# Decoder step: loading x in parallel buffers, taking the statistic of norm 0 before the modulation, and copying pass-through data later

## What is computed

```
mods = (silu(c) @ w_ada + b_ada).reshape(B, 16, 1024)        # 16 vectors per sequence
# layer 0
h = rmsnorm(x, norm_g[0,0]) * (1 + mods[1]) + mods[0]        # "norm 0"
a = h @ w_pw1 + b_pw1;  u = a[:, :1024] * sigmoid(a[:, 1024:])
y = silu(layernorm(depthwise_conv31(concat(state_conv, u)))) @ w_pw2
x = x + mods[2] * y
x = x + mods[5] * swiglu(rmsnorm(x) * (1 + mods[4]) + mods[3])
# then shared keys and values, layer 1: sparse attention and SwiGLU, a last norm
conv_sample = concat(state_conv, u)[:, -30:]                  # its first 22 rows are copies of state_conv
win_sample  = concat(state_win, new rows)                     # its first 256 rows are copies of state_win
```

## Time and profile before

| | us |
|---|---|
| median of 3 runs | 1905.48 (1901.27 to 1909.15) |
| profiled execution, own time | 1907.56 |
| its span | 1905.9 |
| TensorE busy | 1679.4 (88%) |
| VectorE busy | 914.8 (48%) |
| ScalarE busy | 561.5 (29%) |
| GpSimd busy | 270.9 (14%) |

### The profile page before, as it was taken

One profiled execution on the slowest core, in us unless ns is written; L12 is line 12 of the kernel. 1 busy time (PEld: TensorE's weight loads), 2 busy tenths in 40 slices (PEclk: granted clock), 3 DMA queues, 4 the chain that ended last, 5 costly groups with the idle time before them and its releaser, 6 DMA issues.

```text
span 1905.9 us, 30256 instructions
## 1 busy us (share of the span) xinstructions
PE 1679.4 (88%) x12409; PEld 1488.9 (78%) x12409; DVE 914.8 (48%) x1618; ACT 561.5 (29%) x1058; POOL 270.9 (14%) x384
## 2 busy tenths in 40 slices
PE   5788874497999999997988989988897999999995
PEld 2666653397999999997887965454497999999994
DVE  1479999755323232335224246756645323223333
ACT  2332221333222122222221355544423222122222
POOL 1002939120000000000210034432300000000000
PEclk8899987698999999998899999978998999999997
DMA  9399983051233222321322240020221233222311
GB/s 311 157 348 341 307 278 102 0 137 56 78 97 92 66 79 85 107 64 34 100 73 56 77 121 23 1 68 23 67 68 55 78 95 94 63 82 82 110 32 50
DMA packets 236591, 198.10 MB, mean 104 GB/s; under 512 B 6999, under 2 KB 196127, under 8 KB 236253
## 3 DMA queue, kind: packets, MB, share of 16 engines
q1 hardware_dynamic: 230448, 172.54, 29.4%
q0 software_dynamic: 5840, 23.30, 3.9%
q10 hardware_dynamic: 173, 0.39, 0.1%
HBM read 188.88 MB, written 11.20 MB: 105 GB/s over the span
## 4 chain that ended last, share of the span: by engine, by line
PE 71%; DVE 11%; issue 8%; ACT 4%; DMA 3%; DVEq 1%; POOL 1%; SPq 1%; ACTq 0%; POOLq 0%
PE ps L1444 58%; PE ps L1426 4%; PE ps L1752 2%; PE ps L1705 2%; DMA ada<-in_w_ada_dram 2%; DVE y L1117 2%; DVE wl L971 1%; PE ps L1631 1%; DVE r L1117 1%; PE ps L1472 1%; DVE r L995 1%; PE ps L1822 1%; DVE y L1122 1%; PE ps L1607 1%; DVE t L1005 1%
## 5 line engine op out<-in xcount | busy, mean ns | idle before, releaser
L1444 PE MATMUL ps<-Hh,wh 128*128 128x288 f32 x2128 | 470.8, 304 | 67.9 <-DVE Hl L1010 40.8
L1444 PE MATMUL ps<-Hl,wh 128*128 128x288 f32 x2128 | 465.4, 301 | 0.0
L1444 PE MATMUL ps<-Hh,wl 128*128 128x288 f32 x2128 | 464.2, 300 | 0.0
L646 ACT ACTIVATE wh<-raw 128x1024 fp32r<-128x1024 f32 (+1 forms) x173 | 192.9, 1116 | 828.2 <-PE ps L1444 805.8
L1444 PEld LDWEIGHTS ps<-Hh,wh 128*128 128x128 f32 x2128 | 351.5, 194 | 71.9 <-issue 70.5
L1444 PEld LDWEIGHTS ps<-Hl,wh 128*128 128x128 f32 x2128 | 351.9, 193 | 0.2
L1444 PEld LDWEIGHTS ps<-Hh,wl 128*128 128x128 f32 x2128 | 351.5, 193 | 0.2
L971 DVE TENSOR_TENSOR wl<-raw,wh 128x1024 fp32r<-128x1024 f32 (+1 forms) x173 | 225.1, 1301 | 255.5 <-ACT wh L646 255.0
L1444 PE MATMUL ps<-ah,wl 128*128 128x288 f32 x704 | 150.8, 296 | 0.0
L1444 PE MATMUL ps<-ah,wh 128*128 128x288 f32 x704 | 150.8, 296 | 0.0
L1444 PE MATMUL ps<-al,wh 128*128 128x288 f32 x704 | 150.7, 296 | 0.0
(11 more groups left out here) (273 smaller groups left out, 1958.5 us busy)
## 6 DMA issues: line engine op xcount, KB each, us to landing
ada<-in_w_ada_dram SPq DMA_DIRECT2D x64, 1024.0 KB, 7.6
raw<-in_ffn_w_up_dram SPq DMA_DIRECT2D x88, 512.0 KB, 3.8
raw<-in_ffn_w_down_dram SPq DMA_DIRECT2D x32, 704.0 KB, 4.6
raw<-in_conv_w_pw_dram SPq DMA_DIRECT2D x24, 512.0 KB, 8.5
raw<-in_w_kv_dram SPq DMA_DIRECT2D x12, 512.0 KB, 3.7
C<-in_cache_kv_dram POOLq DMA_DIRECT2D x32, 128.0 KB, 4.1
raw<-in_nsa_w_in_dram SPq DMA_DIRECT2D x8, 512.0 KB, 3.8
Cs<-in_cache_kv_dram SPq DMA_DIRECT2D x16, 256.0 KB, 3.9
```

The source lines that it names most:

```text
L646: A(wh[:, u % RING, 0:K, 0:w], raw[:, u % RING, 0:K, 0:w], ACT.Copy).then_inc(hi_ready, 1)
L1444: last = M(ps[0:w, 2 * s + h, 0:HT], wt[:, s, k, 0:w], rt[:, k, h * HT:(h + 1) * HT], start=(k == 0 and i == 0), stop=(k == K - 1 and i == 2))
```

## The change

The x blocks get a buffer each (two in `stage`, three in `xrows`, which lies in the still unused `Hl`), and all five are requested at the start. The two `state_conv` blocks reuse the first two buffers once blocks 0 and 1 are transposed. TensorE transposes the five x blocks in a row, does strip 0, block 5, the eight sums of squares in banks 4 and 5, strip 1 and its turn, block 6, then strips 2 and 3. ScalarE splits units 0 to 2 after the x blocks and squares x after strip 0. It takes the root before the results of strips 2 and 3. VectorE takes the reciprocal of norm 0 before it waits for the modulation. The two pass-through copies are requested behind GpSimd's wait for the first pw2 unit, ahead of the small tables, `w1k`, `w1v` and `C`.

```diff
@@ -94,7 +94,10 @@
...
 STRIPS_FIRST = 4
-STRIP_BLOCKS = [1, 2, 3, 4]
+ROW_BUF = [0, 1, 2, 3, 4, 0, 1]
+ROW_BANK = [0, 1, 2, 0, 1, 0, 1]
@@ -229,6 +232,7 @@
...
         xf = at("xf", [P, DC, T], rH)
+        xrows = at("xrows", [P, 3, D], rH + DC * T * 4)
         rF = region(2 * FHC * T * 4)
@@ -349,6 +353,7 @@
...
         stats = ps[:, 6:8, 0:HT]
+        stats0 = ps[:, 4:6, 0:HT]
@@ -381,6 +386,12 @@
...
         xi_rows = [P, P, P, P, TS, 120, 120]
+        def rows_in(bk):
+            n, k = xi_rows[bk], ROW_BUF[bk]
+            return stage[0:n, k, :] if k < 2 else xrows[0:n, k - 2, :]
         page_rows = a["cache_kv"].rearrange("n (q e) t h d -> n q e (t h d)", e=2)
@@ -493,31 +504,25 @@
...
             def load_rows(bk):
-                n = xi_rows[bk]
-                if bk >= 2:
-                    pool.wait_ge(S("xi_pe"), bk - 1)
+                if bk >= 5:
+                    pool.wait_ge(S("xi_pe"), bk - 4)
                 if bk < 4:
...
                     src = a["state_conv"].rearrange("l b t d -> (l b t) d")[120 * (bk - 5):120 * (bk - 4), :]
-                pool.dma_start(stage[0:n, bk % 2, :], src).then_inc(S(f"xi_in{bk % 2}"), 16)
-            load_rows(0)
-            load_rows(1)
+                pool.dma_start(rows_in(bk), src).then_inc(S(f"xi_in{ROW_BUF[bk]}"), 16)
+            for bk in range(5):
+                load_rows(bk)
             nc.gpsimd.memset(ones[:], 1.0).then_inc(S("const"), 1)
...
             nc.gpsimd.memset(u_p[:, :, 0:CW - 1], 0.0).then_inc(S("const"), 1)
-            for bk in range(2, 7):
+            for bk in range(5, 7):
                 load_rows(bk)
             pool.dma_start(pgt[:], a["page_table"].rearrange("b n -> (b n)").unsqueeze(0)).then_inc(S("pg_in"), 16)
-            pool.dma_start(o["conv_sample"][0, :, 0:CW - 1 - NT, :],
-                           a["state_conv"][0, :, NT:CW - 1, :]).then_inc(S("thru"), 16)
-            pool.dma_start(wss[:, 0:PAST, :], a["state_win"].rearrange("b s t h d -> b s (t h d)")).then_inc(S("thru"), 16)
@@ -546,6 +551,9 @@
...
             pool.wait_ge(ada_ev, 16 * DC)
+            pool.dma_start(o["conv_sample"][0, :, 0:CW - 1 - NT, :],
+                           a["state_conv"][0, :, NT:CW - 1, :]).then_inc(S("thru"), 16)
+            pool.dma_start(wss[:, 0:PAST, :], a["state_win"].rearrange("b s t h d -> b s (t h d)")).then_inc(S("thru"), 16)
             pool.dma_start(w2t[:], a["w_cmp2"].rearrange("t e d -> e t d")).then_inc(S("cb_in"), 16)
@@ -664,7 +672,7 @@
...
                 act.wait_ge(S("st_ck"), sums_done(st))
-                A(halves(r[:]), stats, ACT.Sqrt, scale=1.0 / D, bias=epst[:]).then_inc(S("st_rms"), 1)
+                A(halves(r[:]), stats if st else stats0, ACT.Sqrt, scale=1.0 / D, bias=epst[:]).then_inc(S("st_rms"), 1)
@@ -690,8 +698,6 @@
...
             A(rows0[0:72, 4, :], rows0[0:72, 4, :], ACT.Silu).then_inc(S("c_silu"), 1)
-            for u in range(SPLIT_AHEAD):
-                split_hi(u)
             act.wait_ge(S("vec_pe"), 2)
@@ -699,7 +705,7 @@
...
                 n = xi_rows[bk]
-                src = ps[:, 2 * (bk % 3) + 1, 0:4 * n].rearrange("p (c t) -> p c t", c=4)
+                src = ps[:, 2 * ROW_BANK[bk] + 1, 0:4 * n].rearrange("p (c t) -> p c t", c=4)
                 if bk < 5:
@@ -709,19 +715,21 @@
...
                 block_out(bk)
-                if bk in STRIP_BLOCKS:
-                    if bk == STRIP_BLOCKS[0]:
-                        act.wait_ge(S("vec_dve"), 3)
-                    s_ = STRIP_BLOCKS.index(bk)
-                    strip_out(s_, s_ - 1 if s_ else None)
-            strip_out(None, STRIPS_FIRST - 1)
+            for u in range(SPLIT_AHEAD):
+                split_hi(u)
+            act.wait_ge(S("vec_dve"), 3)
+            strip_out(0, None)
             act.wait_ge(S("xi_dve"), 5)
...
             block_out(5)
+            strip_out(1, 0)
             block_out(6)
             root(0)
+            strip_out(2, 1)
+            strip_out(3, 2)
+            strip_out(None, STRIPS_FIRST - 1)
             norm_hi(0)
@@ -973,6 +981,13 @@
...
                 g0, sh, sc = NORMS[k]
+                def inverse():
+                    dve.wait_ge(S("st_rms"), STAT_OF[k] + 1)
+                    V.reciprocal(r[:], r[:]).then_inc(S("st_r"), 1)
+                if k == 0:
+                    inverse()
                 dve.wait_ge(ada_ev, 2 * max(4 * (sh + 1), 4 * (sc + 1)))
@@ -990,10 +1005,9 @@
...
                                 ALU.mult).then_inc(S("n_s"), 1)
-                if k != 3:
-                    dve.wait_ge(S("st_rms"), STAT_OF[k] + 1)
-                    V.reciprocal(r[:], r[:]).then_inc(S("st_r"), 1)
-                    dve.wait_ge(S("st_r"), STAT_OF[k] + 1)
+                if k not in (0, 3):
+                    inverse()
+                dve.wait_ge(S("st_r"), STAT_OF[k] + 1)
                 dve.wait_ge(S("n_s"), 3 * k + 1)
@@ -1051,12 +1065,13 @@
...
             V.tensor_copy(badaT[:], ps[:, 7, 384:512]).then_inc(S("vec_dve"), 1)
-            for u in range(SPLIT_AHEAD):
-                split_lo(u)
             for bk in range(7):
+                if bk == 5:
+                    for u in range(SPLIT_AHEAD):
+                        split_lo(u)
                 dve.wait_ge(S("xi_pe"), bk + 1)
                 n = xi_rows[bk]
-                src = ps[:, 2 * (bk % 3), 0:4 * n].rearrange("p (c t) -> p c t", c=4)
+                src = ps[:, 2 * ROW_BANK[bk], 0:4 * n].rearrange("p (c t) -> p c t", c=4)
                 if bk < 5:
@@ -1467,9 +1482,9 @@
...
-            def sum_chunk(src, cc, done, n=DC):
+            def sum_chunk(src, cc, done, n=DC, bank=6):
                 for h in range(2):
-                    last = M(ps[:, 6 + h, 0:HT], ones[:], src[:, h * HT:(h + 1) * HT], start=(cc == 0), stop=(cc == n - 1))
+                    last = M(ps[:, bank + h, 0:HT], ones[:], src[:, h * HT:(h + 1) * HT], start=(cc == 0), stop=(cc == n - 1))
                 last.then_inc(done, 1)
@@ -1496,34 +1511,35 @@
...
                 n = xi_rows[bk]
-                pe.wait_ge(S(f"xi_in{bk % 2}"), 16 * (bk // 2 + 1))
-                if bk >= 3:
-                    pe.wait_ge(S("xi_dve"), bk - 2)
-                    pe.wait_ge(S("xi_act"), bk - 2)
+                pe.wait_ge(S(f"xi_in{ROW_BUF[bk]}"), 16 * (1 + bk // 5))
+                if ROW_BANK[bk] in ROW_BANK[:bk]:
+                    before = max(k for k in range(bk) if ROW_BANK[k] == ROW_BANK[bk])
+                    pe.wait_ge(S("xi_dve"), before + 1)
+                    pe.wait_ge(S("xi_act"), before + 1)
                 for cc in range(DC):
-                    last = tr(ps[:, 2 * (bk % 3) + cc // 4, (cc % 4) * n:(cc % 4 + 1) * n],
-                              stage[0:n, bk % 2, cc * P:(cc + 1) * P])
+                    last = tr(ps[:, 2 * ROW_BANK[bk] + cc // 4, (cc % 4) * n:(cc % 4 + 1) * n],
+                              rows_in(bk)[:, cc * P:(cc + 1) * P])
                 last.then_inc(S("xi_pe"), 1)
...
                 block_in(bk)
-                if bk in STRIP_BLOCKS:
-                    s_ = STRIP_BLOCKS.index(bk)
-                    if s_ == 0:
-                        pe.wait_ge(S("const"), 4)
-                        pe.wait_ge(S("vec_act"), 1)
-                        pe.wait_ge(S("vec_dve"), 3)
-                    strip(s_)
-                    if s_:
-                        turn_strip(s_ - 1)
+            pe.wait_ge(S("const"), 4)
+            pe.wait_ge(S("vec_act"), 1)
+            pe.wait_ge(S("vec_dve"), 3)
+            strip(0)
+            block_in(5)
+            pe.wait_ge(S("xi_dve"), 3)
+            pe.wait_ge(S("xi_act"), 3)
+            for cc in range(DC):
+                pe.wait_ge(S("st_sq"), cc + 1)
+                sum_chunk(sqb[:, cc, :], cc, S("st_ck"), bank=4)
+            strip(1)
+            turn_strip(0)
+            block_in(6)
+            for s_ in range(2, STRIPS_FIRST):
+                strip(s_)
+                turn_strip(s_ - 1)
             turn_strip(STRIPS_FIRST - 1)
-            pe.wait_ge(ada_ev, 4 * STRIPS_FIRST)
-            for cc in range(DC):
-                if cc == 2:
-                    block_in(5)
-                    block_in(6)
-                pe.wait_ge(S("st_sq"), cc + 1)
-                sum_chunk(sqb[:, cc, :], cc, S("st_ck"))
             pe.wait_ge(S("st_rms"), 1)
```

## The result

| | median us | runs |
|---|---|---|
| before | 1909.15 | 5 (1901.27 to 1910.40) |
| changed | 1921.61 | 5 (1918.34 to 1924.52) |

The ratio is 1.0076, 95% interval 1.0055 to 1.0097: slower by three quarters of a per cent. The profiled execution has a span of 1922.9 us, 17.0 more than before.

A forecast was written before the change was run, and what follows sets the result against it. The start was taken as bound in turn by transfers, a serial chain and VectorE's taps. 1907.6 - 11.0 + 16.1 + 1.8 = 1914.5 for the profiled execution; the median, 2.1 lower, was named 1913, range 1895 to 1921.

The forecast's parts named there:

- Part 1: First stage: computing the norm statistic ahead of the modulation takes 15.4 us off the path to the dense products.
- The delay of strip 3: First stage: strip 3's last half starts 4.4 us later than before, bounds 1.5 to 8.
- its first term: First stage: 0.6 MB more ahead of `ada` 1 at 387 GB/s makes strip 0 end 1.6 us later.
- Part 3: In pw2: the moved pass-through copies and q0's rest hold back unit 22's weights, so TensorE stands for 16.1 us.
- The gain at the dense products: End of the first stage: first dense product 11.0 us earlier (7.4 to 13.9), from 15.4 - 4.4.
- The memsets and the splits of units 0 to 2 cost nothing: First stage: memsets delayed some 2 us are not waited for before block 0; the splits' first user is the dense product.
- The stall at unit 22: In pw2: weights land near 432.5, are split at 434.8; TensorE, due at 418.7, stands 16.1 us (3 to 22.6).
- The restart: In pw2 after the wait for unit 22: TensorE restarts at the lower clock, costing 1.8 us (0 to 2).
- Rival 1: In pw2: copies stay hidden, unit 22 lands by 410 to 417, stall 0 to 1, time 1894 to 1896; chance 0.17.
- Rival 2: In pw2: stall ends with the large copy, landing 423, stall 6.6, restart 1, time 1902; chance 0.14.
- Rival 3: In pw2: q0's whole rest goes first, landing 437 to 440, stall 21 to 24, time 1917 to 1920; chance 0.18.
- Rival 4: First stage: strips 1 to 3 at lower clock, every load waited for; strip 3 11 late, gain 4, 1919; chance 0.09.

The follow-up runs named there:

- the experiment on what stands behind the copies: Changed kernel with `w1k`, `w1v` and `C` requested only when all pw2 units are done: 1913.46 us, ratio 1.0021 to the kernel before.
- the first experiment: Changed kernel with the two pass-through copies requested when strip 3 has been used, not at the first pw2 unit: 1901.15 us, ratio 0.9952 to the kernel before.

## Why the prediction was wrong

It named 1913 with a range to 1921, and the result was 1921.6, 0.6 beyond. (Its own sum, 1914.5 less 2.1, is 1912.4.) Its profiled execution was forecast at 1914.5 and took 1924.5. The stall and its place were right. The gain of the first stage was too high by 6.6 us, the stall too low by 1.9 and the restart by 1.1: 9.6 of the 10.0 us.

1. *What Part 1 removes*, 15.4 us: measured 15.3. Right.
2. *The delay of strip 3*, taken as 4.4 with bounds 1.5 to 8: measured 10.1. This is the step that failed, and it lay outside its own bounds. Of the missing 5.7 us 5.1 are its first term, the transfers ahead of `ada` 1, where "about half fits into the little-used first 10 us" left 1.6 us: strip 0's second half ran 6.7 us later (30.35 against 23.64). From there on the account fits. It had load 7 requested at 42.8 and landed at about 50; 5.1 us later is 47.9 and 55.1, and the chain has 47.36 and 54.82. The bytes were right: before strip 0's second half q0 moved 3.34 MB, against 2.10, so 1.24 MB more. The sharing was not: from 22 to 26 us `state_conv` took the larger half (0.61 MB of q0, 0.42 of q1), while both together went at 252 to 262 GB/s and not at 387. With `state_conv` later strip 0's second half came 4.7 us earlier than in the changed kernel (25.61). I had used this sharing in Part 3 and not here. The other 3.4 us, put at 2.8, lie behind strip 0, where the sums stand in front of strip 1; moving them brought the dense product forward by 4.1 us against the changed kernel. What bounds the stage was also put too simply: from 20 to 30 us TensorE was busy for 8.20 of the 10 us, and waited 1.80 us for one load.
3. *The gain at the dense products*, 11.0 us: 5.2, and 4.4 by unit 19's split, as the first three units ran 0.65 us longer.
4. *The memsets and the splits of units 0 to 2 cost nothing*: right. The small rows, which I had not counted as held back, came 4.6 us later (14.03, before 9.46). This too cost strip 0 nothing: with them early again its second half stayed at 30.36 (25.42 against 25.61 with `state_conv` late).
5. *The stall at unit 22*, 16.1 us: 18.0. The landing was forecast 33.3 us after the request and took 35.2. Both parts of it stood the test. The large copy ended 24.8 us after the request (forecast 22.3, bound 25.5), and its rest took 10.4 more (forecast 11). *The restart*, 1.8 (0 to 2): 2.9, above its bound.
6. *Rival 1*, the copies hidden in pw2, falls. The reading of the earlier trace rows was right and holds elsewhere: 450 packets of q0 beside 449 of q1. By the rule of the Trainium skill (DMA: Bandwidth & Descriptors, Queues, rings and completion order), a whole run of descriptors per turn, unit 22 would have landed within 18 us of its request, which is an estimate of the forecast. It took 35.2, and no trace here shows such runs between two queues that are both moving. *Rival 2* falls with the experiment on what stands behind the copies. *Rival 3* gave 1917 to 1920 by a stall of 21 to 24; the stall was 18. *Rival 4* had the right place and the right sign (a gain of 4, measured 4.4), with a chance of 0.09. Its condition was half right: strip 3's last half did wait for its load, but most halves of the changed kernel ran at the faster pace (1.07 and 1.06 us at 23.29, 46.24 and 49.22). The cause that it did not name was q0's share of the engines. The case that came is its gain together with the forecast's stall.

The range failed because it took the two terms one at a time: 1919 was rival 4 with the middle of the stall, 1917 to 1920 rival 3 with the middle of the gain.

## What to carry to other kernels

A transfer that nobody waits for is not free: place it by what shares the DMA engines in the next 25 to 35 us, its own queue's rest included. The better of the two places tried with the new first stage was just ahead of 20 us of dense work whose weights were on board, and even there one load landed only 1.1 us before it was needed. The old place was not tried with it. When a chain is shortened by putting work ahead of a step fed by a small ring, check that the work does not keep the ring from being emptied; count bytes of two queues by packets in turn, not by their sum.

## What the runs showed of the hardware

- Two queues that both had packets moving mostly took one packet each in turn, whatever the sizes: 7 and 7 beside 64 KB packets, 18 and 18 beside the copies alone, and 309 and 313, 324 and 325, 450 and 449, 424 and 426 beside mostly 4 KB.
- A load requested while q0 was busy began late. In the kernel before, a weight load was requested at 408.42 us, and up to 413.1 q0 moved 359 packets and q1 none. In the changed kernel unit 22's load was requested at 394.76, and q1 moved nothing up to 399.1. The load requested at 399.16 in the kernel before, beside little traffic, had packets moving by 400.3. Why is open.
- Beside x blocks of 128 rows the two queues together moved 405 GB/s (18 to 20 us of the kernel before, 142 packets of q0 and 144 of q1); beside the blocks of `state_conv`, of 120 rows, 252 to 262. No run here tells why.
- Pieces of 1 KB that one request copied from memory to memory were moved as 4 KB packets: from 400 to 405 us of that run q0 had 349 packets, 1.40 MB.
- The same dense work ran at two paces with the clock granted in full. Windows of 500 to 600 us, of the changed kernel and of the one with the copy over 16 engines:

```profile
500.00:600.00 100.00, 100.00 (x753) 100.00 (x752) 31.43 (x32) 25.25 (x32) 0.00 (x0) 1.00 0.30 87
```

```profile
500.00:600.00 100.00, 100.00 (x771) 100.00 (x770) 31.98 (x33) 26.66 (x33) 0.00 (x0) 1.00 0.32 94
```

The second did 771 matmuls where the first did 753, and won some 11 us between the norms at 450 and 880 us. That execution took 1905 us while the median of its kernel was 1917.5. Single runs 10 us and more below the others occur elsewhere too (1893.69 among 13 of the kernel before, 1886.18 among 7 of the first experiment). What causes it stays open; no verdict above rests on one execution's end time.
